# Splitting the softplus of a stick-breaking attention into two rounded halves, on POOL and DVE, for rounded products with constant matrices

## Chip, cores and metric

One Trainium2 chip, one core of it. The metric is the device time of one execution of the kernel in microseconds, the median of several executions.

## The reference

A first block of two layers (D = 1024, 1024 tokens, f32) feeds a second block. Each layer of the first block mixes four kinds of attention, four heads of 64 channels each. The one that matters here is the stick-breaking attention, with 128-query blocks in the reference and all keys before the query:

```
valid = key_pos[None, :] < q_pos[:, None]
z = einsum('bhqd,bhkd->bhqk', qb, k) * scale
log_keep = where(valid, log_sigmoid(-z), 0.0)
log_tail = cumsum(log_keep, axis=3, reverse=True) - log_keep
w = where(valid, exp(log_sigmoid(z) + log_tail), 0.0)
out = einsum('bhqk,bhkd->bhqd', w, v)
```

The weight of a key is the sigmoid of its score, times what all later keys have left over. Behind the attentions come a gate, an output projection and a layer norm. The rest of the reference (the second block with windowed attention, an RWKV mixer and a feed-forward part) is not touched.

## The kernel before

The program is a chain of stages. Each stage is a block of five instruction streams (PE for TensorE, ACT, DVE, POOL, SP for the DMA queue), each in its own fixed order, tied by semaphores. A stage ends when all of its streams are done. Per layer the stages around the change are: fox attention, `sb_project` (queries, keys, values of the stick-breaking heads), `sb` (`stick_attention`), `latent_project`, `latent_heads`, MLA attention.

Most projections are done with split operands: an f32 matrix is stored as a rounded part (fp32r, which TensorE takes in one pass) and the rounded rest, and `split_gemm` (L202) sums three rounded products (L208). Weight chunks are loaded as f32 and split on POOL by `SplitWeights.split`: a copy that rounds (L193), then a subtraction (L195). The attention products themselves are exact f32 products, which show in the trace as two records each.

`stick_attention` (L588) works on keys times queries. A unit is a pair of heads, one half of the queries (512) and one block of 128 keys; the half that starts at token 0 has 4 key blocks, the other 8, so with 2 pairs of heads there are 24 units per layer. In the four blocks that cross the diagonal of a half the queries before the block are left out, so these units are 512, 384, 256 and 128 queries wide; the other 8 units are 512 wide. Both heads of a unit lie side by side, so vector instructions see 1024, 768, 512 or 256 elements. Per unit:

- PE: scores (L639) of both heads into two banks; the *tails* (L646): the softplus times the constant matrix `minus_later` (-1 for the key itself and all later keys of the block), added onto the scores; the *block sum* (L654): the softplus times a column of ones, which is broadcast to 64 output rows for each head; the weighted sum of the values (L666).
- ACT: Abs (L695), Exp (L697), Ln (L699) give ln(1 + exp(-|z|)); later Exp of the finished logarithms gives the weights (L707), and Exp of minus the block sum gives the share that is kept for earlier keys (L713).
- DVE: softplus = max(z, 0) + that logarithm (L730), in diagonal units a product that zeroes invalid keys (L735) and an added mask before the exponential (L741); the running output is multiplied by the kept share (L748) and gets the unit's sum added (L751), or is copied for the first block (L755).
- POOL does nothing for the units. It splits two weight chunks of the following projection, `C_CQ` at the head of the stage and `C_CKV` when its load has landed.

The order is written out by hand. In step `it`, PE issues the scores of unit `it`, tails and block sum of `it - 1`, the weighted sum of `it - 2`; ACT the three functions of `it`, then both exponentials of `it - 1`; DVE softplus of `it`, the update of the output for `it - 2`, and the diagonal mask of `it`. PE also computes four late value tiles in step 1 (L208), 96 rounded products. Scores have three pairs of banks, softplus two buffers, so softplus of unit u waits for the block sum of u - 2. `project_stage` (L404) runs `latent_project`: 8 token tiles of the chunk `C_CQ` (24 products each), then those of `C_CKV`, while DVE multiplies condition weights that SP loads.

## Time and profile before

| | us |
|---|---|
| median of 3 runs | 3971.34 (3970.75 to 3974.9) |
| the profiled execution | 3972.07 |
| its span | 3970.3 |
| PE busy | 3698.7 (93%) |
| DVE busy | 1727.8 (44%) |
| ACT busy | 1153.5 (29%) |
| POOL busy | 711.9 (18%) |
| granted TensorE clock, mean | 0.97 |

The span is what the profiler saw between the first and the last instruction; the time has 1.8 us more around it. The busy shares are means over many stages with different limits. A matmul's record ends later than TensorE is free for the next, so how long a product really holds TensorE is read from start to start.

### The profile page before, as it was taken

To read this page: it belongs to the slowest core of one execution; us is meant where nothing else is said; L and a number is where in the kernel's file an instruction comes from. 1 tells how busy PE (TensorE), PEld (TensorE's weight loads), DVE (VectorE), ACT (ScalarE), POOL (GpSimd) and SP (SyncE) were. 2 spreads that over 40 slices of the span, in tenths; PEclk is the share of its full clock that TensorE was granted. 3 is DMA by queue.
4 is the path that set the end of the run, shared out by engine and by line. 5 is a ranking of instruction groups with operands and counts; after the bars stand their busy time and mean duration, and the time that the engine had idled before them with its cause. 6 is when DMAs were issued, how large, how long until landed. Compare 5 with 4: busy or idle time off the path is not lost. (4 is left out here: it accounts for less than half of the span.)

```text
span 3970.3 us, 67451 instructions
## 1 busy us (share of the span) xinstructions
PE 3698.7 (93%) x29462; PEld 2799.6 (71%) x29462; DVE 1727.8 (44%) x3002; ACT 1153.5 (29%) x2208; POOL 711.9 (18%) x248
## 2 busy tenths in 40 slices
PE   6899998998999999899889999998999999999998
PEld 5664667886655678779667777776687468787876
DVE  6645546446455454521764545544003252323133
ACT  2436333014363331201644444343110121101011
POOL 2110004121100031221011111110322022323221
PEclk9999899999998999999899999999999999999999
DMA  4121101211211012212110000000222211111112
GB/s 153 53 87 44 60 16 60 87 64 65 75 58 46 22 53 97 108 43 75 51 35 24 25 25 31 25 24 18 82 69 77 85 43 53 43 47 49 42 54 106
DMA packets 190181, 225.67 MB, mean 57 GB/s; under 512 B 20990, under 2 KB 168000, under 8 KB 187080
## 3 DMA queue, kind: packets, MB, share of 16 engines
q1 hardware_dynamic: 189896, 221.47, 16.9%
q8 instruction: 227, 3.72, 0.4%
q14 instruction: 58, 0.48, 0.0%
HBM read 188.89 MB, written 32.56 MB: 56 GB/s over the span
## 5 line engine op out<-in xcount | busy, mean ns | idle before, releaser
L193 POOL CAST weights_high<-weights_value 128x2048 fp32r<-128x2048 f32 x34 | 66.7, 1962 | 1258.9 <-DMA weights_value<-in_w_in_dram 999.1
L208 PE MATMUL banks<-h_high,weights_high 128*128 128x512 f32 x608 | 242.5, 399 | 8.1 <-PEq L830 5.1
L208 PE MATMUL banks<-h_high,weights_low 128*128 128x512 f32 x608 | 239.8, 394 | 0.0
L208 PE MATMUL banks<-ffn_in_high,ffn_weights_high 128*128 128x512 f32 x512 | 205.0, 400 | 7.8 <-PEq L75 7.5
L208 PE MATMUL banks<-ffn_in_low,ffn_weights_high 128*128 128x512 f32 x512 | 204.0, 398 | 0.0
L208 PE MATMUL banks<-ffn_in_high,ffn_weights_low 128*128 128x512 f32 x512 | 203.6, 398 | 0.0
L4281 ACT ACTIVATE hidden_value<-banks 128x512 f32<-128x512 f32 x64 | 38.3, 599 | 556.7 <-PE banks L208 556.6
L208 PE MATMUL banks<-ffn_weights_high,hidden_high 128*128 128x512 f32 x512 | 199.2, 389 | 0.0
L208 PE MATMUL banks<-ffn_weights_low,hidden_high 128*128 128x512 f32 x512 | 199.2, 389 | 0.0
L208 PE MATMUL banks<-ffn_weights_high,hidden_low 128*128 128x512 f32 x512 | 199.2, 389 | 0.0
L208 PE MATMUL banks<-h_high_again,pair_weights_high 128*128 128x512 f32 x384 | 179.4, 467 | 7.1 <-PEq L2318 7.1
L3959 POOL CAST ffn_weights_high<-ffn_weights_value 128x2048 fp32r<-128x2048 f32 x32 | 60.7, 1895 | 632.4 <-DMA ffn_weights_value<-in_w_ff_dram 418.7
L195 POOL TENSOR_TENSOR weights_low<-weights_value,weights_high 128x2048 fp32r<-128x2048 f32 x34 | 161.2, 4741 | 2.7
L4225 DVE TENSOR_TENSOR hidden_value<-hidden_value 128x512 f32<-128x512 f32 x64 | 65.1, 1018 | 215.1 <-ACT hidden_value L4281 215.1
L208 PE MATMUL banks<-weights_high,mixed_high 128*128 128x256 f32 x512 | 148.7, 290 | 8.4 <-PEq L2038 8.4
L208 PE MATMUL banks<-h_split_low,pair_weights_high 128*128 128x512 f32 x384 | 152.5, 397 | 0.0
L850 PE MATMUL banks<-keys,queries 64*128 64x512 f32 (+3 forms) x512 | 107.5, 535 | 48.3 <-ACT attention_scratch L968 42.8
L3961 POOL TENSOR_TENSOR ffn_weights_low<-ffn_weights_value,ffn_weights_high 128x2048 fp32r<-128x2048 f32 x32 | 151.7, 4740 | 2.6
L208 PE MATMUL banks<-h_high_again,pair_weights_low 128*128 128x512 f32 x384 | 150.3, 391 | 0.0
L208 PE MATMUL banks<-weights_high,h_high 128*128 128x256 f32 (+1 forms) x512 | 145.6, 284 | 1.9 <-PEq L625 1.9
L208 PE MATMUL banks<-weights_low,mixed_high 128*128 128x256 f32 x512 | 146.9, 287 | 0.0
L208 PE MATMUL banks<-weights_high,second_low 128*128 128x256 f32 (+1 forms) x512 | 145.7, 284 | 0.0
(481 smaller groups left out, 9158.3 us busy)
## 6 DMA issues: line engine op xcount, KB each, us to landing
ffn_weights_value<-in_w_ff_dram SPq DMA_DIRECT2D x32, 1024.0 KB, 5.4
weights_value<-in_w_in_dram SPq DMA_DIRECT2D x24, 1024.0 KB, 5.3
attention_scratch<-in_ada_w_dram SPq DMA_DIRECT2D x12, 1024.0 KB, 5.3
pair_weights_value<-in_w_in_dram SPq DMA_DIRECT2D x24, 512.0 KB, 3.9
ndow_weights_value<-in_w_in_dram SPq DMA_DIRECT2D x10, 1024.0 KB, 5.2
weights_value<-in_w_out_dram SPq DMA_DIRECT2D x8, 1024.0 KB, 5.4
gates_value<-in_w_in_dram SPq DMA_DIRECT2D x16, 512.0 KB, 4.8
first_mixed<-in_ada_w_dram SPq DMA_DIRECT2D x6, 1024.0 KB, 5.2
```

Source lines behind the costliest of these rows:

```text
L193: nc.gpsimd.tensor_copy(high, value).then_inc(rounded, 1)
L195: nc.gpsimd.tensor_tensor(low, value, high, ALU.subtract).then_inc(done, 1)
L208: mm = nc.tensor.matmul(out, x, y, start=(first and i == 0 and j == 0), stop=(last and i == n - 1 and j == 2))
L850: mm = nc.tensor.matmul(slot(e, at + done, size), q(p, e, t), key(p, e, done * P, (done + size) * P), start=True, stop=turned_part is None)
L3959: nc.gpsimd.tensor_copy(high[:], value[:]).then_inc(rounded, 1)
L3961: nc.gpsimd.tensor_tensor(low[:], value[:], high[:], ALU.subtract).then_inc(split, 1)
L4225: nc.vector.tensor_tensor(place(hid_value, g), place(hid_value, g), place(hid_value, g), ALU.mult).then_inc(squared, 1)
L4281: nc.scalar.activation(place(hid_value, g), k.bank(g % 4), ACT.Relu).then_inc(moved, 1)
```

## The change

Softplus is split, like other operands, into a rounded half and a rounded rest, and the two sums over keys become rounded products.

- POOL, which used to be idle after the weight split, waits for each unit's softplus and copies it to `softplus_high` (fp32r). Before that it rounds the constant matrices once per stage: `later_sign` from `minus_later`, and `one_sign`, 256 columns whose two halves put the sum of one head on rows 0 to 63 or 64 to 127 and zeros on the other rows.
- DVE subtracts it from the softplus into `softplus_low`, in place of the f32 softplus, behind the update of the output and before the diagonal mask.
- PE waits for that subtraction. Tails are four rounded products per unit (two heads, high and low), and so is the block sum, all four into one bank.
- POOL no longer splits `C_CKV` in this stage. `latent_project` does it at its head.

```diff
-def stick_attention(k, name, qt, kt, values, out, z_bufs, sp_bufs, p_bufs, keep_bufs, w=None, splits=(), late=(), late_load=None):
+def stick_attention(k, name, qt, kt, values, out, z_bufs, sp_bufs, p_bufs, keep_bufs, rounded_bufs, w=None, splits=(), late=(),
+                    late_load=None):
...
             def do_tails(u):
-                pe.wait_ge(softplus_ready, u + 1)
+                if u == 0:
+                    pe.wait_ge(signs_ready, 2)
+                pe.wait_ge(split, u + 1)
                 for e in range(2):
-                    mm = nc.tensor.matmul(logs(u)[:, e, :], k.minus_later, part(sp_bufs, u)[:, e, :], start=False, stop=True,
-                                          skip_group_check=True)
+                    for x, bufs in enumerate((high_bufs, low_bufs)):
+                        mm = nc.tensor.matmul(logs(u)[:, e, :], later_sign, part(bufs, u)[:, e, :], start=False, stop=(x == 1),
+                                              skip_group_check=True)
                 mm.then_inc(tails, 1)
...
                 for e in range(2):
-                    mm = nc.tensor.matmul(k.psum[half_rows[e], 6, first[u]:HALF], k.one[:, 0:1].broadcast_to([P, 64]),
-                                          part(sp_bufs, u)[:, e, :], start=True, stop=True)
+                    for x, bufs in enumerate((high_bufs, low_bufs)):
+                        mm = nc.tensor.matmul(k.psum[:, 6, first[u]:HALF], one_sign[:, e * P:(e + 1) * P], part(bufs, u)[:, e, :],
+                                              start=(e == 0 and x == 0), stop=(e == 1 and x == 1))
                 mm.then_inc(block_summed, 1)
...
         @block.gpsimd
         def _(pool):
-            if splits:
-                w.split(pool, splits, st.sem("weights_rounded"), st.sem("weights_split"))
+            nc.gpsimd.tensor_copy(later_sign, k.minus_later).then_inc(signs_ready, 1)
+            for e in range(2):
+                nc.gpsimd.tensor_copy(one_sign[:, 192 * e:192 * e + 64], k.one[:, 0:1].broadcast_to([P, 64]))
+            nc.gpsimd.tensor_copy(one_sign[:, 64:192], k.before01[:, 0:1].broadcast_to([P, P])).then_inc(signs_ready, 1)
+            w.split(pool, splits, st.sem("weights_rounded"), st.sem("weights_split"))
+            for u in range(N):
+                pool.wait_ge(softplus_ready, u + 1)
+                if u >= 2:
+                    pool.wait_ge(block_summed, u - 1)
+                nc.gpsimd.tensor_copy(part(high_bufs, u), part(sp_bufs, u)).then_inc(rounded, 1)
...
+            def low(u):
+                dve.wait_ge(rounded, u + 1)
+                nc.vector.tensor_tensor(part(low_bufs, u), part(sp_bufs, u), part(high_bufs, u), ALU.subtract).then_inc(split, 1)
+
...
                 if it >= 2:
                     add(it - 2)
+                if it < N:
+                    low(it)
                 if it < N and diagonal[it]:
                     mask_diagonal(it)
...
+        softplus_high = k.over("softplus_high", [P, 2, S], heads_at + 6 * S * 4)
+        softplus_low = k.over("softplus_low", [P, 2, S], scratch_at + 2 * S * 4)
+        later_sign = k.sb("later_signs", [P, P], F32R, ctx=own)
+        one_sign = k.sb("one_signs", [P, 2 * P], F32R, ctx=own)
...
-                    [qt[:, 2, i * HALF:(i + 1) * HALF] for i in range(2)], splits=(C_CQ, C_CKV), w=W,
+                    [qt[:, 2, i * HALF:(i + 1) * HALF] for i in range(2)], b.softplus_split, splits=(C_CQ,), w=W,
...
-        project_stage(k, "latent_project" + tag, groups, W, lead_sp=lead_sp, then_wait=[(arrived, 160)], nbanks=7, rider=rider,
+        project_stage(k, "latent_project" + tag, groups, W, lead_sp=lead_sp, splits=(C_CKV,), then_wait=[(arrived, 160)], nbanks=7, rider=rider,
```

The line numbers move by a few: scores are L641, tails L651, block sum L660 and the weighted sum L672 in the changed kernel; softplus is L744, its masking L749, the subtraction L754, the diagonal mask L759, the update L766 and L769 or L773, POOL's copy L698.

DVE, steps of three off-diagonal full-width units in the second half of the queries, before (`attention_scratch` written by L730 is the softplus, `first_mixed` the running output of the first layer, `queries` holds the kept share):

```order
L730 SCALAR_TENSOR_TENSOR attention_scratch<-banks,attention_scratch 128x1024
L748 TENSOR_TENSOR first_mixed<-first_mixed,queries 128x128
L751 TENSOR_TENSOR first_mixed<-first_mixed,banks 128x128
L730 SCALAR_TENSOR_TENSOR attention_scratch<-banks,attention_scratch 128x1024
L755 COPY first_mixed<-banks 128x512
L730 SCALAR_TENSOR_TENSOR attention_scratch<-banks,attention_scratch 128x1024
L748 TENSOR_TENSOR first_mixed<-first_mixed,queries 128x512
L751 TENSOR_TENSOR first_mixed<-first_mixed,banks 128x512
```

The same place in the changed kernel:

```order
L744 SCALAR_TENSOR_TENSOR attention_scratch<-banks,attention_scratch 128x1024
L766 TENSOR_TENSOR first_mixed<-first_mixed,queries 128x128
L769 TENSOR_TENSOR first_mixed<-first_mixed,banks 128x128
L754 TENSOR_TENSOR softplus_low<-attention_scratch,softplus_high 128x1024
L744 SCALAR_TENSOR_TENSOR attention_scratch<-banks,attention_scratch 128x1024
L773 COPY first_mixed<-banks 128x512
L754 TENSOR_TENSOR softplus_low<-attention_scratch,softplus_high 128x1024
L744 SCALAR_TENSOR_TENSOR attention_scratch<-banks,attention_scratch 128x1024
L766 TENSOR_TENSOR first_mixed<-first_mixed,queries 128x512
L769 TENSOR_TENSOR first_mixed<-first_mixed,banks 128x512
L754 TENSOR_TENSOR softplus_low<-attention_scratch,softplus_high 128x1024
```

Each softplus is followed by the update of an earlier unit, and only then by the new subtraction.

TensorE, one full-width unit of the same run, before (scores, tails, block sum, weighted sum):

```order
L639 MATMUL banks<-queries,keys 128x512 x2
L646 MATMUL banks<-attention_scratch,masks_and_identity 128x512 x2
L654 MATMUL banks<-attention_scratch,one 64x512 x2
L666 MATMUL banks<-attention_scratch,values 64x512 x2
```

and in the changed kernel (`later_signs` and `one_signs` are the rounded constants):

```order
L641 MATMUL banks<-queries,keys 128x512 x2
L651 MATMUL banks<-softplus_high,later_signs 128x512
L651 MATMUL banks<-softplus_low,later_signs 128x512
L651 MATMUL banks<-softplus_high,later_signs 128x512
L651 MATMUL banks<-softplus_low,later_signs 128x512
L660 MATMUL banks<-softplus_high,one_signs 128x512
L660 MATMUL banks<-softplus_low,one_signs 128x512
L660 MATMUL banks<-softplus_high,one_signs 128x512
L660 MATMUL banks<-softplus_low,one_signs 128x512
L672 MATMUL banks<-attention_scratch,values 64x512 x2
```

The order of the four kinds is kept; the two in the middle have twice as many products, and the block sum is 128 rows wide instead of 64.

## Rows read from the trace of the kernel before

**Rows 1.** Windows, both stages (layer 1, then layer 0) and a part: us, PE, PEld, DVE, ACT, POOL busy, clock, DMA.

```profile
1044.00:1164.00 120.00, 107.99 (x480) 47.13 (x480) 63.21 (x104) 88.35 (x121) 12.89 (x4) 0.94 0.05 9
...
256.00:376.00 120.00, 108.90 (x481) 47.92 (x482) 63.21 (x104) 88.36 (x121) 12.88 (x4) 0.94 0.05 9
...
276.00:300.00 24.00, 20.73 (x80) 8.12 (x80) 14.45 (x18) 17.57 (x24) 6.40 (x2) 0.86 0.04 5
```

**Rows 2.** Timeline, layer 0, full-width run: start us, us, engine, line, out<-in, [idle before].

```profile
296.26 1.06 ACT L699 ACTIVATE attention_scratch<-attention_scratch 128x1024 f32<-128x1024 f32 x1
...
297.41 1.23 DVE L730 SCALAR_TENSOR_TENSOR attention_scratch<-banks,attention_scratch 128x1024 f32<-128x1024 f32 x1 [2.85 <-ACT attention_scratch L699]
...
298.93 1.98 PE L646 MATMUL banks<-attention_scratch,masks_and_identity 128*128 128x512 f32 x4
...
300.85 1.08 PE L654 MATMUL banks<-attention_scratch,one 128*64 128x512 f32 x4
...
302.71 1.13 PE L639 MATMUL banks<-queries,keys 64*128 64x512 f32 x4
...
303.77 1.98 PE L646 MATMUL banks<-attention_scratch,masks_and_identity 128*128 128x512 f32 x4
...
303.89 1.02 ACT L695 ACTIVATE attention_scratch<-banks 128x1024 f32<-128x1024 f32 x1 [0.24 <-PE banks L639]
...
306.03 1.06 ACT L699 ACTIVATE attention_scratch<-attention_scratch 128x1024 f32<-128x1024 f32 x1
```

**Rows 3.** Timeline, layer 0, diagonal units of the second half.

```profile
311.01 0.43 DVE L741 TENSOR_TENSOR banks<-banks,masks_and_identity 128x256 f32<-128x256 f32 x1 [0.83 <-PE banks L646]
...
311.35 0.95 DVE L730 SCALAR_TENSOR_TENSOR attention_scratch<-banks,attention_scratch 128x768 f32<-128x768 f32 x1
...
312.33 0.42 DVE L735 TENSOR_TENSOR attention_scratch<-attention_scratch,masks_and_identity 128x256 f32<-128x256 f32 x1
...
312.67 0.68 DVE L748 TENSOR_TENSOR first_mixed<-first_mixed,queries 128x512 f32<-128x512 f32 x1
...
313.33 1.56 PE L646 MATMUL banks<-attention_scratch,masks_and_identity 128*128 128x384 f32 x4
...
315.00 0.43 DVE L741 TENSOR_TENSOR banks<-banks,masks_and_identity 128x256 f32<-128x256 f32 x1 [0.92 <-PE banks L646]
...
318.13 0.43 DVE L741 TENSOR_TENSOR banks<-banks,masks_and_identity 128x256 f32<-128x256 f32 x1 [0.26 <-PE banks L646]
...
321.06 0.43 DVE L741 TENSOR_TENSOR banks<-banks,masks_and_identity 128x256 f32<-128x256 f32 x1 [0.66 <-PE banks L646]
```

**Rows 4.** Groups by line and shape, POOL and DVE: xcount | busy us, mean ns | idle before.

```profile
L3722 POOL CAST ranch_weights_high<-branch_weights 128x1024 fp32r<-128x1024 f32 x8 | 8.3, 1039 | 107.0 <-DMA branch_weights<-in_w_branch_dram 107.0
...
L193 POOL CAST weights_forget_high<-weights_forget_value 128x256 fp32r<-128x256 f32 x2 | 0.8, 396 | 32.7 <-DVE x_residual L1482 23.0 <-DMA weights_forget_value<-in_w_in_dram 9.7
...
L2845 DVE TENSOR_TENSOR window_queries_keys<-window_queries_keys,ention_out_channel_major 128x1024 f32<-128x1024 f32 x12 | 14.6, 1214 | 0.0
```

**Rows 5.** Timeline, TensorE, rounded products of 512 columns in a projection.

```profile
236.38 0.40 PE L208 MATMUL banks<-h_high,weights_high 128*128 128x512 f32 x1
...
236.62 0.40 PE L208 MATMUL banks<-second_low,weights_high 128*128 128x512 f32 x1
```

**Rows 6.** Timeline, layer 0: the split of the second latent chunk beside a diagonal unit.

```profile
279.92 4.51 POOL L195 TENSOR_TENSOR weights_low<-weights_value,weights_high 128x2048 fp32r<-128x2048 f32 x1
...
280.12 4.59 DVE L735 TENSOR_TENSOR attention_scratch<-attention_scratch,masks_and_identity 128x256 f32<-128x256 f32 x1
...
284.77 1.22 PE L646 MATMUL banks<-attention_scratch,masks_and_identity 128*128 128x128 f32 x4 [3.26 <-DVE attention_scratch L735]
```

**Rows 7.** Timeline, layer 0: tails of a full-width unit after a wait.

```profile
340.76 3.15 PE L646 MATMUL banks<-attention_scratch,masks_and_identity 128*128 128x512 f32 x4 [2.06 <-DVE attention_scratch L730]
```

**Rows 8.** Timeline, layer 0: TensorE and DVE at the head of the latent projection.

```profile
375.78 0.55 PE L208 MATMUL banks<-weights_high,h_high 128*128 128x256 f32 x1 [0.94 <-PEq L625]
...
390.83 0.62 DVE L390 TENSOR_SCALAR keys<-first_mixed,condition_silu 128x256 f32<-128x256 f32 x2 [15.60 <-DMA first_mixed<-in_ada_w_dram]
```

More of the change, by code:

```diff
@@ L599, in stick_attention @@
     names = ("scores_done", "abs_ready", "exp_ready", "log_ready", "softplus_ready", "tails_summed", "diagonal_ready", "weights_ready",
-             "block_summed", "kept_ready", "summed", "added", "faded", "masked")
+             "block_summed", "kept_ready", "summed", "added", "faded", "masked", "softplus_rounded", "softplus_split", "signs_ready")
     (scores_done, abs_ready, exp_ready, log_ready, softplus_ready, tails, diagonal_ready, weights_ready,
-     block_summed, kept_ready, summed, added, faded, masked) = (st.sem(n) for n in names)
+     block_summed, kept_ready, summed, added, faded, masked, rounded, split, signs_ready) = (st.sem(n) for n in names)
+    high_bufs, low_bufs, later_sign, one_sign = rounded_bufs
     units = [(p, half, b) for p in range(2) for half in range(2) for b in range(4 * half + 4)]
@@ L1125, in first_block @@
             b.h_high, b.mixed_high, b.gate_sigmoids = h_high, mixed_high, gate_sigmoids
+            b.softplus_split = [[x[:, i, :] for i in range(2)] for x in (softplus_high, softplus_low)] + [later_sign[:], one_sign[:]]
             b.x, b.mixed, b.mixed_low = (one_value, one_mixed, one_low) if n == 0 else (two_value, two_mixed, two_low)
```

## The prediction

> **What bounds the kernel now.** I read the windows first, for the stick-breaking stage of each layer, because that is the only stage whose instructions change. It takes some 120 us twice [rows 1]: 240 of the 3970.3 us. TensorE (PE) is busy for 108.9 of the 120 us, ACT for 88.4, DVE for 63.2, POOL for 12.9, and TensorE's clock is at 0.94 of full on the mean. So TensorE looks like the bound, with ACT some way behind. But a busy share does not say which wait ends last, so I then went to the timeline of the stage.
>
> In a run of full-width units (both heads, 512 queries) the tails product of L646 starts at 298.93 and again at 303.77: 4.84 us per unit, with TensorE passing from L646 to L654, L666, L639 and back with no gap [rows 2]. Under it lies a ring that is nearly as long. The Ln of one unit ends at 297.32 (296.26 + 1.06), then come softplus on DVE (L730), tails (L646), block sum (L654), the weighted sum (L666), the scores of the unit two further on (L639), and Abs, Exp and Ln of that unit on ACT, which end at 307.09. That is 9.77 us for two units, 4.88 each, and in all of it only 0.29 us is slack, between the end of L730 (298.64) and the start of L646. **A later start of the tails is paid by this ring at once.**
>
> In the units that cross the diagonal the ring is shorter and tighter: mask the scores (L741), softplus of the next unit (L730), zero its invalid part (L735), tails (L646), mask again. L741 follows L741 after 3.99 us for the unit of 384 queries, 3.13 for 256, 2.93 for 128 [rows 3]. Of the 24 units of a stage 12 are 512 wide (8 of them off the diagonal), 4 are 384, 4 are 256 and 4 are 128.
>
> **The change part by part.** *The products.* Tails: two exact f32 products of 512 columns are four records and take 1.92 us (298.93 to 300.85) [rows 2]. The new ones are four rounded products of 512 columns, which elsewhere follow each other by 0.235 us (236.38 to 236.62) [rows 5]: 0.94 us, 0.98 less. Block sum: the two f32 products of 64 output columns ran side by side and held TensorE for about 0.9 us; the four rounded ones are 128 wide, so they run one after the other, 0.94 us: no gain. TensorE's work per full unit falls from 4.84 to some 3.9 us.
>
> *The way to them.* Between softplus and tails there are now a POOL copy of 1024 elements and a DVE subtraction. The copy has the form of L3722, 1.04 us (0.40 for 256 elements, so about 0.83 and 0.61 between); the subtraction, two SBUF operands of 1024, that of L2845, 1.21 us [rows 4] (0.95, 0.68 and 0.42 for the narrow ones, in proportion to the rows of rows 3). I add 0.1 us for each of the two handovers, since the row-to-row handovers seen go up to that (303.77 for TensorE's end to 303.89 on ACT) [rows 2].
>
> *The place in DVE's queue.* The subtraction stands behind the update of the output (L748, L751) of two units earlier, and L748 has two SBUF operands. The trace shows what such an instruction and a POOL instruction do to each other: a POOL subtraction started at 279.92 and ran 4.51 us, and L735, which takes 0.42 elsewhere, took 4.59 from 280.12 on; TensorE then stood 3.26 us [rows 6]. In the new order L748 is issued straight behind softplus, ahead of POOL's copy, so I let the copy start only when L748 is done, 0.68 us later [rows 3]. The Trainium skill (SBUF — State Buffer, section on who interferes with whom) states the same as a rule: a DVE instruction with two SBUF inputs and a GpSimd instruction that reads SBUF exclude each other for a whole instruction, and the first to issue has its way. The trace agrees, with those 4.59 us. Without the exclusion, an overlap of the two would take 0.34 us from each full unit and 0.55 to 0.68 from each narrow one, 11.7 us per layer.
>
> *The sum per layer.* Full units, per ring of two: in go 0.68 + 1.04 + 1.21 + 0.2 = 3.13, less the slack of 0.29, less 0.98 of tails, plus 0.04 of block sum: +1.90, or +0.95 per unit, x12 = **+11.4**. The four on the diagonal I price alike. Narrow units, ring of one, 384 wide: mask to softplus 0.34, softplus 0.98, L735 0.42, L748 0.68, copy 0.83, subtraction 0.95, handovers 0.2, tails 0.70, handover 0.1 = 5.20 against 3.99: +1.21. For 256: 0.34 + 0.72 + 0.42 + 0.68 + 0.61 + 0.68 + 0.2 + 0.47 + 0.1 = 4.22 against 3.13: +1.09. For 128, where L748 works on 384 columns (0.55) and four products are taken at the price of four of 256: 0.34 + 0.44 + 0.42 + 0.55 + 0.40 + 0.42 + 0.2 + 0.47 + 0.1 = 3.34 against 2.93: +0.41. Together 2.71, x4 = **+10.8**.
>
> *The moved weight split.* POOL's split of the second latent chunk (copy and the 4.51 us subtraction) leaves the stage, and with it the stall of rows 6: **-3.3**. It now starts at the head of the latent projection. There TensorE starts at 375.78 and needs that chunk only after 8 token tiles of 24 products, near 0.12 each, some 22 us later; DVE stands until 390.83 for a DMA [rows 8]. The 6.4 us of POOL lie in that shade: 0. If that cover were gone the price would be those 6.4 us. The four small copies of the constants (an estimate of 1 us from the 0.40 of rows 4) and the first chunk's split keep POOL for about 7.5 us at the head of the stage, where TensorE has the 96 late value products before it, some 11 us at half of 0.235 each: 0.
>
> *The clock.* TensorE worked at 1.2 GHz after its longer waits: behind the 3.26 us of rows 6 the stretch 276 to 300 has a clock of 0.86 [rows 1], and behind a wait of 2.06 us the four records of L646 took 3.15 instead of 1.98 us [rows 7]. Over the stage 0.94 means 14 of 120 us at that level. With 3.9 us of work in units of 5.8 us, TensorE waits before nearly every tails product. As an estimate I let the share at 1.2 GHz grow from 0.12 to 0.29 of a stage of some 138 us: 40 us. TensorE's steps are two thirds of the ring (3.9 of 5.8) and double there, so a microsecond at that level costs 0.33: 13.2 against 4.8 before, **+8.4**. The Trainium skill (TensorE: Matmul & The Clock Gate, section on why this matters for your kernels) ties the fall to idle gaps of a certain length between bursts of matmuls. If all waits stay shorter than that, this term is 0, which is the first rival.
>
> Sum per layer 11.4 + 10.8 - 3.3 + 8.4 = 27.3 us, for two layers +54.6. The profiled execution took 3972.07 us (span 3970.3), 0.7 above the median of 3971.34: **4026 us** against that median. POOL and DVE do 27 and 25 us more work per layer; neither is the bound by its sum, only by its place.
>
> **The rivals.** (1) *The ring lengthens but the clock stays as it is.* For it: the waits are 2 us each, and the shortest of the rows after which the clock fell was 2.06. Against it: they come in every unit. Then +18.9 per layer: 4009 us. (2) *The copy overlaps L748.* Against it stand rows 6, though they show a POOL subtraction, not a copy. 18.9 - 11.7 = 7.2, with some of the clock term 13: 3998 us. (3) *The handovers to and from POOL are slower*, 0.3 instead of 0.1 us, and half of the stage is at 1.2 GHz: some 10 us more per layer: 4045 us. (4) *Faster.* The copy and the subtraction are hidden, and TensorE's relief counts. The mechanism is the ring of rows 2: it shortens if what is put in between L730 and L646 is less than the 0.29 of slack and the 0.98 of tails, 1.27 us. Then ACT is the bound of a full unit: 1.02, 1.06 and 1.06 [rows 2], and, as an estimate from these, one more of that width and one of half, 4.78 with the gaps, a gain of 0.06 x12; the narrow rings lose 0.8, 0.6 and 0.2 of tails, x4 = 6.4; the stall goes, 3.3: -10.4 per layer, 3950 us. For it speaks that TensorE is busy 91% of the stage [rows 1]; against it that copy and subtraction alone are 2.25 us and wait for each other. (5) *The rounded products cost as much as exact ones.* Then eight of them per unit take 7.7 us and TensorE is the bound at about 9.7 us; rows 5 leave nothing of it.
>
> **How the numbers follow.** Forecast 0.64, rival 1 0.12, rival 2 0.08, rival 3 0.10, rival 4 0.05, rival 5 and anything unseen 0.01. A measurement of this kernel tells about 0.2%, 8 us, from no change. Faster by more than that: 0.05, rival 4. Within it: 0.03, which is a mix of rivals 2 and 4. Slower: 0.92. The range of 3997 to 4044 takes in rivals 1 and 2 at its foot and nearly all of rival 3.
>
> **What would show it.** Right: in the profile after, full units come every 5.6 to 6.5 us, L773/L769 and the new subtraction (L754) wait for POOL, the copy (L698) has a mean above 1.04 us or starts only behind L766, TensorE waits for L754 before L651 for some 40 us per layer, the stage takes 140 to 150 us, and its clock falls to 0.8 or 0.85. The latent projection is as long as before. Wrong: units at 4.8 us with ACT busy throughout (rival 4), a clock that stays at 0.94 (rival 1), a copy that runs beside L766 (rival 2), or any stage outside these two that changes its length.

## The result and the profile after

The changed kernel takes 4023.5 us (median of 4 runs, 4017.52 to 4027.09) against 3971.05 (3970.52 to 3974.9): 1.0131 times as long, interval 1.0119 to 1.0144. The forecast was 4026 us. The profiled execution took 4017.52 us, its span is 4015.7. POOL is busy 762.2 us instead of 711.9, DVE 1764.4 instead of 1727.8, and TensorE 3683.7, 15 us less than before in a kernel that takes 52 us longer by the medians.

From here on "the stage" runs from the start of the first scores to the start of the last weighted sum. Windows, layer 0 then layer 1, of the kernel before (columns as in [rows 1]):

```profile
256.00:374.60 118.60, 108.45 (x480) 47.67 (x480) 62.92 (x103) 88.36 (x121) 12.88 (x4) 0.94 0.05 9
1045.20:1163.00 117.80, 107.66 (x478) 47.02 (x480) 62.87 (x103) 88.31 (x121) 12.86 (x4) 0.94 0.05 9
```

and of the changed kernel:

```profile
256.00:403.90 147.90, 108.74 (x480) 62.57 (x480) 81.37 (x127) 88.76 (x121) 31.76 (x30) 0.85 0.04 8
1071.10:1214.10 143.00, 103.44 (x480) 60.64 (x480) 81.38 (x127) 89.03 (x121) 31.75 (x30) 0.89 0.04 8
```

The stages grew from 236.4 to 290.9 us, by 29.3 and 25.2: 54.5 in all. TensorE is busy as long as before in a longer stage, and its clock fell from 0.94 to 0.85 and 0.89. A clock of 0.85 on the mean of the two levels, 1.2 and 2.4 GHz, is 30% of the time at the lower one; so 44 and 31 us against 14 each. The windows give the clock to two digits, which leaves such figures open by some 1.5 us.

What TensorE waits for is the new subtraction, and the copy ahead of it has become longer than an undisturbed one. From the view of the instructions of L754 (who waited: us in both layers, times):

```profile
L754 DVE TENSOR_TENSOR softplus_low<-attention_scratch,softplus_high x48: 424/1092/1227, 267.1 to 1211.0; 128x1024 fp32r<-128x1024 f32 x24, 128x768 fp32r<-128x768 f32 x8, 128x512 fp32r<-128x512 f32 x8, 128x256 fp32r<-128x256 f32 x8
...
  PE banks L651: 77.2, 43
```

from the same views of the kernel before, first of L730, then of L735, which were the last to write what its tails read:

```profile
  PE banks L646: 4.1, 2
...
  PE banks L646: 14.2, 10
```

and from the groups by shape of the changed kernel in layer 0:

```profile
L698 POOL CAST softplus_high<-attention_scratch 128x1024 fp32r<-128x1024 f32 x12 | 14.4, 1203 | 62.4 <-DVE attention_scratch L744 38.8 <-DVE attention_scratch L749 23.6
```

TensorE's products stood 77.2 us in both layers for L754, 38.6 per layer, where they had stood 18.3 in both for the softplus. Before the copies POOL sits idle most of the time; its share of the span says nothing about the harm.

The timeline of full-width units, the place of [rows 2] (idle before in brackets):

```profile
300.39 1.04 POOL L698 CAST softplus_high<-attention_scratch 128x1024 fp32r<-128x1024 f32 x1 [8.63 <-DVE attention_scratch L744]
...
301.53 1.23 DVE L754 TENSOR_TENSOR softplus_low<-attention_scratch,softplus_high 128x1024 fp32r<-128x1024 f32 x1 [0.61 <-POOL softplus_high L698]
...
302.81 0.79 PE L651 MATMUL banks<-softplus_high,later_signs 128*128 128x512 f32 x1 [2.86 <-DVE softplus_low L754]
...
303.40 0.63 PE L651 MATMUL banks<-softplus_low,later_signs 128*128 128x512 f32 x1
...
303.83 0.63 PE L651 MATMUL banks<-softplus_high,later_signs 128*128 128x512 f32 x1
...
304.73 0.68 DVE L766 TENSOR_TENSOR first_mixed<-first_mixed,queries 128x512 f32<-128x512 f32 x1
304.88 1.43 POOL L698 CAST softplus_high<-attention_scratch 128x1024 fp32r<-128x1024 f32 x1 [3.45 <-DVE attention_scratch L744]
...
306.19 1.08 PE L672 MATMUL banks<-attention_scratch,values 128*64 128x512 f32 x4
...
307.39 0.69 DVE L769 TENSOR_TENSOR first_mixed<-first_mixed,banks 128x512 f32<-128x512 f32 x1 [1.98 <-PE banks L672]
308.11 1.22 DVE L754 TENSOR_TENSOR softplus_low<-attention_scratch,softplus_high 128x1024 fp32r<-128x1024 f32 x1
...
309.39 0.50 PE L651 MATMUL banks<-softplus_high,later_signs 128*128 128x512 f32 x1 [1.06 <-DVE softplus_low L754]
...
311.45 1.08 PE L672 MATMUL banks<-attention_scratch,values 128*64 128x512 f32 x4
```

Three things are to be seen. First, behind the wait of 2.86 us the rounded products follow each other by 0.43 us (303.40 to 303.83), not by the 0.235 of [rows 5]: the lower clock. Second, a copy with L766 in front of it takes 1.43 instead of 1.04 us, 0.39 more. Third, and the prediction has no price for this: that copy ended at 306.31, but the subtraction started only at 308.11. It stands in DVE's queue behind L769, which waits for the weighted sum of L672. That closes a ring of one unit: subtraction to tails 1.28 (301.53 to 302.81), tails to weighted sum 3.38, weighted sum to L769 1.20, L769 to the next subtraction 0.72: 6.58 us from tails to tails (302.81 to 309.39). It does not bind in every unit: by the views of their instructions L769 waited for the weighted sum in 18 of 40 updates, 25.4 us in both layers, and L754 for POOL's copy in 19 of 48, 9.8 us.

All full units cost more, not only those of the timeline. From one softplus to the next, by the starts of L730 and of L744, the eight off-diagonal ones of a layer took 40.9 and 41.0 us before and take 53.0 and 48.8 now, 6.6 and 6.1 each. The four on the diagonal went from 19.6 and 19.3 to 26.2 and 26.3.

The diagonal units, the place of [rows 3], mask to mask, with DVE's queue in the unit of 256 queries, and the head of the latent projection, as in [rows 8]:

```profile
318.30 0.43 DVE L759 TENSOR_TENSOR banks<-banks,masks_and_identity 128x256 f32<-128x256 f32 x1 [2.17 <-PE banks L651]
...
323.63 0.43 DVE L759 TENSOR_TENSOR banks<-banks,masks_and_identity 128x256 f32<-128x256 f32 x1 [1.06 <-PE banks L651]
...
325.03 0.69 DVE L766 TENSOR_TENSOR first_mixed<-first_mixed,queries 128x512 f32<-128x512 f32 x1
...
325.18 1.01 POOL L698 CAST softplus_high<-attention_scratch 128x512 fp32r<-128x512 f32 x1 [3.85 <-DVE attention_scratch L749]
...
325.75 0.69 DVE L769 TENSOR_TENSOR first_mixed<-first_mixed,banks 128x512 f32<-128x512 f32 x1
...
326.47 0.69 DVE L754 TENSOR_TENSOR softplus_low<-attention_scratch,softplus_high 128x512 fp32r<-128x512 f32 x1
...
327.22 0.39 PE L651 MATMUL banks<-softplus_high,later_signs 128*128 128x256 f32 x1 [1.50 <-DVE softplus_low L754]
...
328.00 0.43 DVE L759 TENSOR_TENSOR banks<-banks,masks_and_identity 128x256 f32<-128x256 f32 x1 [0.83 <-PE banks L651]
...
405.21 1.90 POOL L193 CAST weights_high<-weights_value 128x2048 fp32r<-128x2048 f32 x1 [5.50 <-POOLq L627]
405.24 0.55 PE L208 MATMUL banks<-weights_high,h_high 128*128 128x256 f32 x1 [0.95 <-PEq L627]
...
407.19 4.58 POOL L195 TENSOR_TENSOR weights_low<-weights_value,weights_high 128x2048 fp32r<-128x2048 f32 x1
...
420.28 0.62 DVE L390 TENSOR_SCALAR keys<-first_mixed,condition_silu 128x256 f32<-128x256 f32 x2 [15.60 <-DMA first_mixed<-in_ada_w_dram]
```

5.33 us for the unit of 384 queries and 4.37 for 256, where 3.99 and 3.13 stood. Here too the subtraction stands behind L769: the copy ended at 326.19, L769 at 326.44, and the subtraction started at 326.47. The moved split ends at 411.77, long before its chunk is used, and DVE waits for the same DMA as before, by the same 15.60 us: it costs nothing there.

### The profile page after: what moved, and what is told of

It is laid out like the page before. It is cut to its first block and busy times, and to the rows that moved or that the text cites. A ratio compares the mean times of both kernels' runs of the same rounds, so it can differ in the third digit from the quotient of the medians.

```text
span 4015.7 us, 67625 instructions
## 1 busy us (share of the span) xinstructions
PE 3683.7 (92%) x29462; PEld 2822.5 (70%) x29462; DVE 1764.4 (44%) x3050; ACT 1155.0 (29%) x2208; POOL 762.2 (19%) x304
```

## The experiments

Each was run beside the kernel before on the same chip; the ratios are against that. The medians of before were 3969.35, 3972.45 and 3968.74 us. Times of one kernel spread by some 10 us, so I also compare the stages.

**The chain without the cheap products** (`e1`). The copy and the subtraction stay, the products are the exact ones of the unsplit softplus. The subtraction writes over the high half, which nothing reads.

```diff
-                        mm = nc.tensor.matmul(logs(u)[:, e, :], later_sign, part(bufs, u)[:, e, :], ...
+                    mm = nc.tensor.matmul(logs(u)[:, e, :], k.minus_later, part(sp_bufs, u)[:, e, :], ...
...
-                nc.vector.tensor_tensor(part(low_bufs, u), part(sp_bufs, u), part(high_bufs, u), ALU.subtract).then_inc(split, 1)
+                nc.vector.tensor_tensor(part(high_bufs, u), part(sp_bufs, u), part(high_bufs, u), ALU.subtract).then_inc(split, 1)
```

> The changed kernel with the copy on POOL and the subtraction on DVE kept (the subtraction writes over the rounded half, and nothing reads it), but tails and block sum as exact products of the unsplit softplus, as before; TensorE still waits for the subtraction. Theory of the ring (the time sits between softplus and tails): worse than the changed kernel by what the products had given back, 0.98 us per ring of two full-width units and 0.9, 0.6 and 0.2 us per narrow unit, 12.6 us per layer at full clock; TensorE is busier, so its clock stays higher and takes some 4 us of that back. Stage 153 to 158 us, time 4023 + 2 x 8 = 4036 to 4048 us. Rival (the rounded products or the wider block sum are what costs): back to the time of the kernel before, 3965 to 3975 us.

4036.75 us (4029.0 to 4046.76), 1.0169 [1.0145, 1.0194]. The way to the products costs 67 us over before, although the moved split, which `e3` will price at 5 us, is in it; the rounded products give back 13 of the 67. Its stages are 151.4 and 153.8 us with the clock at 0.93 and 0.91, together 14.3 longer than after although the clock is higher.

**The cheap products without the chain** (`e2`). DVE writes the softplus rounded at once; there is no copy and no subtraction. The low half is left out and the high half is multiplied twice, so TensorE's work is that of the change.

```diff
-                pe.wait_ge(split, u + 1)
+                pe.wait_ge(softplus_ready, u + 1)
...
-                    for x, bufs in enumerate((high_bufs, low_bufs)):
+                    for x, bufs in enumerate((high_bufs, high_bufs)):
...
-                nc.gpsimd.tensor_copy(part(high_bufs, u), part(sp_bufs, u)).then_inc(rounded, 1)
...
-                sp = part(sp_bufs, u)
+                sp = part(high_bufs, u)
```

> The changed kernel with DVE's softplus written rounded at once, no copy on POOL and no subtraction on DVE; the eight rounded products per unit stay, each pair taking the rounded half twice (the rest is left out, and the half counts twice). Theory of the ring: nothing is put in between softplus and tails, tails are 0.98 us shorter and the stall by the weight split is gone, so the stage falls under that of the kernel before, to some 109 us, and the time to about 3950 us, as in the rival that ended faster. Rival (the products cost): 4010 to 4030 us, as the changed kernel.

3944.54 us (3941.44 to 3950.68), 0.9935 [0.9918, 0.9951]. Windows of its two stages:

```profile
255.90:362.80 106.90, 94.72 (x480) 55.57 (x480) 58.97 (x103) 86.83 (x121) 7.32 (x6) 0.97 0.05 10
1035.90:1140.70 104.80, 92.61 (x480) 54.39 (x480) 58.95 (x103) 86.84 (x121) 7.31 (x6) 0.98 0.05 11
```

24.7 us less in the two stages than before, 79.2 less than after. Some 6 of the 24.7 are the moved split (`e3` below has stages of 116.1 and 114.2 us), the other 18.6 come with the cheaper products. So the gain on TensorE is real, and the whole loss is in the step that makes the two halves, with the waits and the clock that it brings.

**The clock** (`e4`). TensorE does eight products of 256 columns whose result nobody reads, ahead of its wait for the subtraction.

```diff
+                if u >= 2:
+                    pe.wait_ge(kept_ready, u)
+                    for i in range(8):
+                        nc.tensor.matmul(k.psum[:, 6, 0:256], later_sign, one_sign, start=True, stop=True)
                 pe.wait_ge(split, u + 1)
```

> The changed kernel with eight products of 256 columns of constants (0.95 us) in front of TensorE's wait for the subtraction, from the third unit on; their result is overwritten. They add nothing else and lie in time in which TensorE waited. Theory with the clock term (+8.4 us per layer of the 27.3): the stage stays at 2.4 GHz nearly throughout and shortens by 6 to 10 us, time 4003 to 4012 us. Rival (the clock's fall is free because TensorE is not what the stage waits for): same or a little slower, 4020 to 4030 us.

4014.97 us (4008.26 to 4022.19), 1.0119 [1.0098, 1.014]. Windows of its stages, and two of its tails (L655 is L651 of the change):

```profile
255.50:393.20 137.70, 120.64 (x655) 78.57 (x656) 81.29 (x127) 88.88 (x121) 31.84 (x30) 0.96 0.04 8
1064.70:1201.70 137.00, 119.99 (x656) 77.92 (x656) 81.32 (x127) 88.87 (x121) 31.84 (x30) 0.96 0.04 8
```

```profile
300.11 0.50 PE L655 MATMUL banks<-softplus_high,later_signs 128*128 128x512 f32 x1 [0.78 <-DVE softplus_low L758]
...
305.59 0.50 PE L655 MATMUL banks<-softplus_high,later_signs 128*128 128x512 f32 x1
```

With more work on TensorE the stages are 10.2 and 6.0 us shorter. The clock is at 0.96, 8% of the stage or 11 us at the lower level, so 33 and 20 us fewer than after: some 0.3 us for each of them. From tails to tails the same unit takes 5.48 us at full clock. The median of the whole kernel is only 8.5 us under that of the change, a miss of the expectation, and the two intervals overlap: on the whole kernel the gain isn't clear of noise, and what this run shows it shows by its stages. The mean clock of the whole execution hints at why: 0.967 after and 0.972 here are 265 and 224 us at 1.2 GHz, of which 75 and 22 lie in the stages, so outside them it is 190 and 202, each open by up to 7 us by the rounding. So the execution after may have had a little less of it elsewhere.

**A second copy** (`e7`). POOL copies each softplus twice, one behind the other.

```diff
+                nc.gpsimd.tensor_copy(part(high_bufs, u), part(sp_bufs, u)).then_inc(copied_once, 1)
+                pool.wait_ge(copied_once, u + 1)
                 nc.gpsimd.tensor_copy(part(high_bufs, u), part(sp_bufs, u)).then_inc(rounded, 1)
```

> The changed kernel with POOL's copy of the softplus done twice, the second after the first. It doubles a suspected cost. Theory of the ring: the copy is on the ring whole, so a full-width unit takes 0.5 us more and a narrow one 0.8, 0.6 or 0.4, 12 x 0.5 + 4 x 1.85 = 14 us per layer and, with a few more falls of the clock, up to 17: 4051 to 4058 us. Rival (the copy is hidden and DVE's subtraction alone makes the time): 4023 to 4030 us.

4066.92 us (4064.9 to 4069.57), 1.0246 [1.0229, 1.0263], 43 us over after, more than either expectation: a miss.

```profile
256.60:418.80 162.20, 109.58 (x480) 64.17 (x480) 81.22 (x127) 89.12 (x121) 51.68 (x54) 0.85 0.04 7
1090.70:1254.90 164.20, 111.58 (x479) 64.29 (x480) 81.33 (x127) 89.33 (x121) 51.69 (x54) 0.84 0.04 7
```

The stages took 35.5 us more. Second copies are 19.9 us per layer by their means in the groups by shape (12 of 1.04, 4 each of 0.83, 0.62 and 0.40), 39.8 in both. But the two layers tell different things. Layer 0 has the clock of 0.85 that it had after, and is 14.3 us longer: the 14 of the expectation, where a full unit pays for half a copy and a narrow one for a whole one. Layer 1 is 21.2 longer with the clock down from 0.89 to 0.84, some 21 us more at 1.2 GHz; these are worth some 6 at the price above, which leaves 15. The other 8 of the 43 us lie outside the stages. So POOL is on the path, at 19% of the span, but not for all of its time.

**The subtraction ahead of the update** (`e5`). Now neither L766 nor L769 stands between softplus and subtraction.

```diff
-                if it >= 2:
-                    add(it - 2)
                 if it < N:
                     low(it)
+                if it >= 2:
+                    add(it - 2)
```

> The changed kernel with DVE's subtraction issued ahead of the update of the output, so that neither the multiplication with two SBUF operands nor the wait for the weighted sum stands between softplus and subtraction; DVE now waits for POOL's copy instead of updating meanwhile. Theory that the place in DVE's queue costs: 0.4 to 0.7 us less between softplus and tails where a multiplication stood in front, but the update now lies in front of the next softplus in narrow units, so half of it comes back: 1 to 4 us less per layer, time 4015 to 4022 us, and the copy's mean falls to its undisturbed 1.04 us at full width. Rival (the shared port is a small matter): 4020 to 4027 us, with the copies as short as in the first case.

4021.34 us (4016.32 to 4025.24), 1.0135 [1.0111, 1.0159]: no difference from the change that these runs can tell. Yet the order did what it should. A group by shape, the full-width copies of layer 0, and the timeline of the same two units:

```profile
L698 POOL CAST softplus_high<-attention_scratch 128x1024 fp32r<-128x1024 f32 x12 | 12.5, 1040 | 66.3 <-DVE attention_scratch L744 38.8 <-DVE attention_scratch L749 27.5
```

```profile
301.92 0.79 PE L651 MATMUL banks<-softplus_high,later_signs 128*128 128x512 f32 x1 [2.85 <-DVE softplus_low L754]
...
305.13 1.22 DVE L754 TENSOR_TENSOR softplus_low<-attention_scratch,softplus_high 128x1024 fp32r<-128x1024 f32 x1 [1.14 <-POOL softplus_high L698]
...
305.63 1.98 PE L672 MATMUL banks<-attention_scratch,values 128*64 128x512 f32 x4
...
307.54 1.29 PE L641 MATMUL banks<-queries,keys 64*128 64x512 f32 x4
...
308.75 0.50 PE L651 MATMUL banks<-softplus_high,later_signs 128*128 128x512 f32 x1
```

The copies are back at 1.04 us, and the subtraction was done at 306.35, 4.43 us behind the last tails, where after needs 6.52 (302.81 to 309.33). But TensorE took from 301.92 to 308.75 for eight rounded products, a weighted sum and scores, nearly all at 1.2 GHz, without a wait for the subtraction. In this unit TensorE itself is the bound at the lower clock, with 6.83 us. The stages had the clock at 0.83 and 0.87, lower than after, and took 146.5 and 140.8 us. In the narrow units the update now stands ahead of the mask instead.

**The copy on DVE** (`e6`, on top of `e5`).

```diff
-                nc.gpsimd.tensor_copy(part(high_bufs, u), part(sp_bufs, u)).then_inc(rounded, 1)
...
+                nc.vector.tensor_copy(part(high_bufs, u), part(sp_bufs, u)).then_inc(rounded, 1)
```

> The kernel of the run before this one (subtraction ahead of the update) with the rounding copy on DVE instead of POOL: no handover and no other engine at the port. Theory of the ring: what counts is the length of what is put in between, 1.04 us of copy and two handovers become one DVE copy of 0.6 to 1.0 us without handovers, so 6 to 8 us less per layer, time 4005 to 4012 us although DVE has more to do. Rival (DVE's load bounds the stage, and POOL was the right place): 4025 us or more.

4012.54 us (4004.14 to 4020.82), 1.0117 [1.009, 1.0143]. From the groups by shape, layer 0:

```profile
L749 DVE CAST softplus_high<-attention_scratch 128x1024 fp32r<-128x1024 f32 x12 | 8.3, 694 | 0.4
```

0.69 us instead of 1.04 and no handover to another engine. The stages take 140.3 and 136.6 us, 10.4 less than `e5` and 14.0 less than the change in both; the intervals of the times still overlap.

**The weight split back in the stage** (`e8`). POOL splits the second chunk between the copies of units 3 and 4 instead of in the latent projection.

```diff
+                if u == 4:
+                    w.split(pool, (late_load,), weights_rounded, weights_split, first=1)
...
-        project_stage(k, "latent_project" + tag, groups, W, lead_sp=lead_sp, splits=(C_CKV,), then_wait=[(arrived, 160)], nbanks=7, rider=rider,
+        project_stage(k, "latent_project" + tag, groups, W, lead_sp=lead_sp, then_wait=[(arrived, 160)], nbanks=7, rider=rider,
```

> The changed kernel with the split of the second latent chunk back in the stage, between the copies of the units 3 and 4. Theory: the move was needed, since the split of 6.4 us now stands in front of a copy on the ring and in front of DVE's two-operand instructions; it delays that unit's tails by some 5 to 6.4 us, plus a stretch at 1.2 GHz: 5 to 7 us more per layer, 4033 to 4037 us. Rival (it would have been hidden, as nothing waits for POOL there): 4020 to 4027 us.

4026.96 us (4024.86 to 4027.87), 1.0144 [1.0121, 1.0167]: a miss, 3.5 us over the change and not 10, and with intervals that overlap nothing that can be told from it. Timeline (L757 is L754 of the change, L701 its copy, L747 its softplus):

```profile
281.30 1.89 POOL L193 CAST weights_high<-weights_value 128x2048 fp32r<-128x2048 f32 x1
...
282.41 1.05 DVE L757 TENSOR_TENSOR softplus_low<-attention_scratch,softplus_high 128x256 fp32r<-128x256 f32 x1
283.27 4.59 POOL L195 TENSOR_TENSOR weights_low<-weights_value,weights_high 128x2048 fp32r<-128x2048 f32 x1
...
287.00 1.22 DVE L747 SCALAR_TENSOR_TENSOR attention_scratch<-banks,attention_scratch 128x1024 f32<-128x1024 f32 x1 [1.77 <-ACT attention_scratch L716]
...
288.29 1.16 POOL L701 CAST softplus_high<-attention_scratch 128x1024 fp32r<-128x1024 f32 x1 [0.42 <-DVE attention_scratch L747]
```

The 4.59 us of POOL lay in the one long gap of DVE, where it waits for the next full-width scores, logarithms and all, and POOL was free again (287.86) before the next copy was due. Only L757, 1.05 instead of 0.42, met a POOL instruction. The softplus at 287.00, which reads a bank and one SBUF operand, ran its usual 1.22 us beside POOL for 0.86 us. The Trainium skill (SBUF — State Buffer, section on who interferes with whom) says that a DVE instruction with at most one SBUF input, outside the modes that use two ports, doesn't contend with GpSimd; the trace agrees, with that 1.22.

**Only the split moved** (`e3`), on the kernel before; 12 runs.

```diff
-                    [qt[:, 2, i * HALF:(i + 1) * HALF] for i in range(2)], splits=(C_CQ, C_CKV), w=W,
+                    [qt[:, 2, i * HALF:(i + 1) * HALF] for i in range(2)], splits=(C_CQ,), w=W,
...
+        project_stage(k, "latent_project" + tag, groups, W, lead_sp=lead_sp, splits=(C_CKV,), then_wait=[(arrived, 160)], nbanks=7, rider=rider,
```

> The kernel before with the second chunk's weight split moved to the latent projection and nothing else. Theory as in the prediction: the stall of DVE behind POOL goes, 3.3 us per layer, and the split is hidden at its new place: about 3964 to 3966 us. Rival: the gain is smaller, because the kernel before is bound by TensorE right behind the stall or other waits at 1.2 GHz take the place: 3968 to 3972 us.

3963.34 us (3958.78 to 3967.23), 0.9983 [0.9975, 0.9992]: 5.4 us less than before. That is the part of the change that helps by itself.

**Scores earlier** (`e9`, on top of `e3`, exact products). TensorE issues the scores of unit u + 2 straight behind the tails of u, ahead of the block sum and the weighted sum.

```diff
                 mm.then_inc(tails, 1)
+                if u + 2 < N:
+                    do_scores(u + 2)
...
-                if it < N:
+                if it < 2:
                     do_scores(it)
```

> The run before this one with TensorE's scores of the unit two further on issued behind the tails instead of in front of the next tails. Theory: TensorE no longer works on scores when the next softplus is ready, which shortens the narrow rings a little: 2 to 3 us per layer less than the kernel before, 3961 to 3967 us. Rival (TensorE's sum of work bounds the stage whatever the order): as the run before this one.

3951.94 us (3948.06 to 3956.36), 0.9956 [0.9944, 0.9969]. It leaves nothing out and beats both kernels, by 17 and by 72 us; more than I expected. Windows of `e3`, then of `e9`:

```profile
257.10:373.20 116.10, 107.27 (x480) 47.28 (x480) 58.82 (x103) 88.22 (x121) 6.43 (x2) 0.96 0.05 10
1046.70:1160.90 114.20, 105.32 (x480) 45.91 (x480) 58.85 (x103) 88.13 (x121) 6.43 (x2) 0.97 0.05 10
```

```profile
256.30:369.70 113.40, 106.26 (x479) 46.99 (x480) 58.88 (x103) 87.35 (x121) 6.47 (x2) 0.97 0.05 10
1039.00:1149.80 110.80, 103.70 (x478) 45.48 (x480) 58.86 (x103) 87.25 (x121) 6.52 (x2) 0.98 0.05 10
```

6.1 of the 11.4 us to `e3` lie in the stages. The others lie outside, where nothing was edited. The executions of `e9` have a mean clock of mostly 0.974, those of `e3` of mostly 0.972, which is some 16 us less at 1.2 GHz; at 0.3 us each that would be about as much, but no run tests it.

**The high half alone** (`e10`): `e2` with each product once, four per unit. The rounded rest of the softplus is left out, so the two sums are computed from rounded values.

```diff
-                    for x, bufs in enumerate((high_bufs, high_bufs)):
-                        mm = nc.tensor.matmul(logs(u)[:, e, :], later_sign, part(bufs, u)[:, e, :], ...
+                    mm = nc.tensor.matmul(logs(u)[:, e, :], later_sign, part(high_bufs, u)[:, e, :], ...
```

> Softplus written rounded by DVE at once, and only this half used: four rounded products per unit instead of eight, no copy, no subtraction. It leaves the rounded rest of the softplus out of both sums. Theory: TensorE has some 2.9 us of work per full unit, so ACT with 4.8 us is what bounds the full units, and the narrow rings lose the tails' second half: 0 to 4 us per layer less than the run with eight products at 3944.5 us: 3937 to 3945 us; more stretches at 1.2 GHz may take all of that back. Rival (TensorE still bounds): 12 x 0.9 = 11 us per layer less, 3923 us.

3941.8 us (3938.93 to 3951.11), 0.9938 [0.9918, 0.9959]. Half of the products less, and nothing measurable to `e2`. Its stages are 103.8 and 101.2 us, 6.7 less in both, where TensorE as the bound would have given 22: there it is not the bound. **With the scores earlier** (`e11`, the edit of `e9` on `e10`):

> The kernel that uses the rounded half alone, with the same new order of TensorE. It leaves the rounded rest out too. Theory: the ring of full-width units loses the block sum and the weighted sum, but ACT bounds them already: 0 to 2 us per layer less, 3938 to 3942 us. Rival (ACT waits for the kept share behind the later block sum): 2 to 5 us per layer more.

3943.48 us (3938.23 to 3948.27), 0.9937 [0.9924, 0.995]. A miss: no gain. What bounds these two wasn't followed up; ACT is busy 86 of some 103 us.

## Why the prediction was right, step by step

*The stages.* 54.6 us were forecast, 54.5 came. The profiled execution, at 45.5 us over that of before, got 9 us back outside the stages; the medians differ by 52.4. That the two agree to 0.1 us is luck; the terms are checked one by one below.

*The ring without the clock and without the split*: 11.4 + 10.8 = 22.2 us per layer. The pair of runs that bears on it is `e4` against `e3`: both have the split moved, and both have the clock at 0.96 or 0.97. Their stages differ by 21.6 and 22.8 us, 22.2 on the mean. From softplus to softplus, by the starts in the timelines, the full units account for 11.1 and 12.3, the narrow ones for 11.8 and 12.0, and the head of the stage is 1.3 and 1.4 shorter. Against the kernel before `e4` is 19.1 and 19.2 us longer, with 18.9 set. The products of `e4` itself are in these figures, so they hold only as far as those lie in waits; in the unit of its timeline the tails start right behind the subtraction.

*The clock*: +8.4. Between `e4` and the change lie 10.2 and 6.0 us, 8.1 on the mean. The share was 0.30 and 0.22 against 0.29, the price some 0.3 against 0.33 per microsecond. That the clock is the cause of this part is shown by `e4`, by two stages of one execution each. With the clock near that of before, the stages of `e4` are what rival 1 set.

*The copy behind L766*: a step that was mis-sized. 0.68 were set, and 0.39 were measured (1.43 against 1.04). The copy starts its record 0.15 us behind that of L766 and ends 0.90 behind L766's end, 0.14 less than the 1.04 of a copy: part of its start lies under L766. [rows 6] has the same 0.14: L735, which takes 0.42, ended 0.28 behind POOL's subtraction. Rival 2, a free overlap, is refuted by the same rows.

*What was missed*: the subtraction waits in DVE's queue behind L769. The prediction saw the update ahead of the subtraction, but counted only the 0.68 of its first half. In the narrow units L769 puts back what the copy was over-priced by: from L766 to the subtraction it is 1.44 us in the unit of 256 queries (325.03 to 326.47), where 0.68 + 0.61 + 0.2 = 1.49 were set for L748, copy and handovers. So this part of the sum came out right for a reason that the prediction didn't have; that is luck. The units took 5.33 and 4.37 against 5.20 and 4.22, the rest of it in the way from tails to mask, 0.78 (327.22 to 328.00) where 0.57 were set. That is the tails and their handover, 0.21 under-priced. In full units the wait of L769 for the weighted sum is added. The ring that it closes was 6.58 us where part of it ran at the lower clock; at full clock its pieces, with tails to weighted sum at 2.06 (309.39 to 311.45), give 5.26, below the 5.79 of the forecast ring. With the clock up, in `e4`, L769 waited 10.0 us in 10 updates of both layers instead of 25.4 in 18. So this ring binds mostly where the clock has fallen, and how much of the 54.5 us it makes is open: `e5` took it out and gained nothing measurable, and in the unit shown the next bound was TensorE at the lower clock.

*The stall by the split*: -3.3 per layer, and `e3` measured -5.4 in both, -2.7 each. `e8`, with the split at another place of the stage, shows no such price. *The latent projection*: unchanged, as said. The forecast also wanted L769 and the subtraction to wait for POOL; L769 waited for the weighted sum alone, and the subtraction for POOL only 9.8 us. Its 27 and 25 us of added work for POOL and DVE don't follow from its own rows, which give some 21 and 23; measured were 25.2 and 18.3 per layer, and nothing hung on them.

*Rival 4* named its condition, that less than 1.27 us be put in between. `e2` meets it and gives 3944.5, where 3950 was set. *Rival 3*, slower handovers, is refuted: L754 starts 0.10 us behind the copy's end (301.43 to 301.53). *Rival 5* is refuted by the 2.06 us that eight products take at full clock, not 7.7.

## What to carry to other kernels

Before you make an engine's work cheaper, lay out the ring that feeds it. Cheaper products gave back 13 us here, and making their operands cost 67, though POOL and DVE were at 19% and 44%. A new instruction in an in-order queue inherits every wait ahead of it, so read what the instruction in front of it waits for. And in a ring with waits the clock adds to the loss, and the cheap work at the low clock can become a bound of its own, as in the unit shown of `e5`.

## What the runs showed of the hardware

Extra products that nobody reads made the stages shorter: 10.2 and 6.0 us, by a clock of 0.96 in place of 0.85 and 0.89. A rounding copy of 1024 elements takes 0.69 us on DVE and 1.04 on POOL. A POOL copy that started 0.15 us behind a DVE instruction with two SBUF operands ended 0.90 us behind it, not 1.04. The spread of one kernel goes with the clock: the 17 executions of the kernel before beside `e3` run from 3963.4 us at a mean clock of 0.972 to 3974.9 at 0.968. That is 11.5 us for some 32 more at 1.2 GHz, near the 0.3 or so that a microsecond cost in the stages. So differences under some 10 us between single executions mean little here without the clock beside them.
